# Step orders of their own for each layer and the first head pair, and earlier gate evictions, in a two-layer hybrid decoder trunk

## The chip, the cores and the metric

The kernel runs on one core of one Trainium2 chip. The metric is the device time of one execution in microseconds (us). A core has five engines that run side by side and wait for each other by semaphores: TensorE (PE, matmuls and transposes), VectorE (DVE), ScalarE (ACT), GpSimd (POOL) and SyncE (SP, which here issues the weight transfers).

## What is computed

The trunk has two layers over 528 tokens, 16 meta tokens ahead of 512, with 1024 channels.

```python
for l in range(DEPTH):
    u = rms_norm(h, norm_mix[l])
    glu_in, q, k, v, gates = jnp.split(u @ w_in[l], SPLITS, axis=-1)
    a = (glu_in + b_glu[l]); a = a[..., :C_CONV] * jax.nn.sigmoid(a[..., C_CONV:])
    a = causal_depthwise_conv(a, conv_w[l], conv_b[l])              # 31 taps
    y_conv = jax.nn.silu(layer_norm(a, ...)) @ w_pw[l] + b_pw[l]
    q, k = (apply_rope(rms_norm(x), cos, sin) for x in (q, k))      # 8 heads x 2 components x 64
    o = diff_attention(q, k, v, lam)          # softmax(q0 k0) - lam * softmax(q1 k1), causal, times v
    y_attn = rms_norm(o, subln[l], SUBLN_EPS) * (1.0 - lam_init)
    g_conv, g_attn = jnp.split(gates, 2, axis=-1)
    h = h + (jax.nn.sigmoid(g_conv) * y_conv + jax.nn.sigmoid(g_attn) * y_attn) @ w_o[l]
    u = rms_norm(h, norm_mlp[l])
    h = h + jnp.square(jax.nn.relu(u @ w_up[l])) @ w_down[l]
```

## The kernel before

For more precision than one matmul gives, weights and activations are split into a high and a low part, and each product is three matmuls (high x high, high x low, low x high). GpSimd makes the low parts of the weight slabs (`w_lo`), and in the attention stages ScalarE the high ones (`w_hi`).

A layer runs in this order: the GLU (`A_GLU`); then five **stages** of attention; then the gates and the layer norm of the convolution; then the pointwise product (`A_PW`), the output product (`A_O`) and the MLP. Stage 0 has only the projection tiles of v, q and k for head pair 0. Stages 1 to 4 do the attention of head pair 0 to 3; stages 1 to 3 also hold the projection tiles of the next pair, and stage 4 holds the first eight of the 16 gate tiles. Below, "first" is stage 1, "middle" are stages 2 and 3, "last" is stage 4. Layer 0 has 15 projection tiles a stage (five token tiles of v, q and k), layer 1 has 14, since the meta tokens' queries are not needed there.

The names of the steps, in which the change is written, with h0 and h1 the two heads of the stage's pair:

- `tile` (T): one projection tile; T< and T> are its first and second half, between which other steps may stand. ScalarE evicts it (`b_evict`) where its second half stands in the order: v to `v_sb`, q and k to `raw` with their squares. Behind the eviction of the last tile of v, of q and of k ScalarE casts the high part of the slab after the next (`w_high_part`, L871), GpSimd subtracts (`split_low`, L503).
- `gate` (G): a quarter of a gate tile. The first eight use one bank pair in turn; each must be evicted by VectorE (`gate`, `sg`, L1227) before the next starts. Gate tiles 8 to 15, in the normalisation, alternate between two bank pairs.
- `q`, `k` (k0, k1): transposes of the roped q and k, evicted by ScalarE (high part) and VectorE (low part, `qk_evict`). GpSimd makes the first product of the rope (`turn`, L548 and L549), VectorE the rest (`rope`; rq and rk in the new tables), behind the statistics (`rope_stats`).
- `s` (s00, s01, s02 for h0, s10 to s12 for h1): scores of a group of query tiles; `m` their maxima on VectorE (`maxima`), `e` the exponentials on ScalarE. The next scores wait for the exponentials of those before, since they use the same banks.
- `c` (`combine`, L1167): VectorE subtracts the second softmax from the first, in SBUF.
- `t` (t00, t01, t10, t11): transposes of the combined matrix, evicted to `a_t` by ScalarE (L906); the second half reuses the banks of the first.
- `pv`: its product with v. ScalarE sums its squares, VectorE scales it (`subln`), and `y` is its transpose. `pv-`, `y-` and `sub-` belong to the head before.

TensorE, ScalarE and VectorE each run their steps strictly in the order in which they are written. `schedule(layer, stage)` gives the order of TensorE and ScalarE, from a table of positions (`after`: an even key is the middle of a tile, an odd one its end) that serves stages 1 to 3 of both layers alike. VectorE's order is written out in its block. Between the steps it works off the taps of the convolution that the GLU has left (`some_taps(n)`, L441, 182 of them a layer), one multiply-and-add over 512 tokens each; `ln_sums` behind the last tap releases the layer norm's sums. In the normalisation VectorE multiplies each of eight channel tiles (L1405), ScalarE applies silu and VectorE subtracts its high part (`silu_lo`, L1135).

Of the kernel before, what the change touches and what calls it, by code (L numbers as in the profile page):

```python
# [40 lines left out]
T = META + SEQ  # L41
# [127 lines left out]

def schedule(layer, stage):  # L170

    h0, h1, pair = 2 * stage - 2, 2 * stage - 1, stage - 1
    pv = [("pv", h0 - 1)] if stage > 1 else []
    y = [("y", h0 - 1)] if stage > 1 else []
    s = lambda h, n: [("s", h, n)]
    e = lambda h, n: [("e", h, n)]
    if stage == 4:  # L180
# [47 lines left out]
def build(nc, x_t, w_slabs, pvecs, rows_in, ident_in, mask_in, identb_in, out, h_spill):  # L228
    ctx = ExitStack()
    with ctx:  # L230
# [834 lines left out]
        def _(dve):  # L1065
# [167 lines left out]
            for layer in range(LAYERS):  # L1233
# [89 lines left out]
                for stage in range(5):  # L1323
                    h0, h1 = 2 * stage - 2, 2 * stage - 1
                    last = stage == 4
                    if stage == 0:
                        some_taps(30)
                        rope(layer, 0, 0)
                        some_taps(8)
                        continue  # L1330
# [7 lines left out]
                    some_taps(1)  # L1338
                    qk_evict(layer, stage - 1, "q")
                    some_taps(1)  # L1340
                    qk_evict(layer, stage - 1, "k", 0)
                    maxima(layer, h0, 0)
                    if last:
                        gate(layer, 1)
                        some_taps(1)
                        maxima(layer, h0, 1)
                        qk_evict(layer, 3, "k", 1)
# [20 lines left out]
                        for _ in taps:  # L1368
                            pass
# [167 lines left out]
```

How the kernel before makes its waits and increments, by code:

```python
    def mark(self, ins):  # L104
        ins.then_inc(self.sem, 1)
        self.n += 1
# [1 line left out]
    def link(self, ins, back=0):  # L108
        self.mark(ins)
        if self.off is not None or self.n > back:
            self.eng.wait_ge(self.sem, self.value(back))
# [9 lines left out]
def announce(eng, ins, sem, value):  # L122
    ins.then_inc(sem, 1)
    eng.wait_ge(sem, value)
# [257 lines left out]
        def a_wait(eng, layer, slab, tile, k, col):  # L383
            if col == 0:
                eng.wait_ge(a_full, k + ((layer * A_TILES + tile) // 2 + 1))
            else:
                eng.wait_ge(w_used, k + (layer * SLABS + slab + 1))
# [5 lines left out]
        def b_read_wait(eng, n):  # L394
            for k in range(2):
                eng.wait_ge(b_free[k], (n + 1 - k) // 2)
# [1 line left out]
        def round_wait(eng, n):  # L399
            for m in (n - 1, n):
                eng.wait_ge(t_free[m % 2], m // 2 + 1)
# [1 line left out]
        def pv_read_wait(eng, layer, hh):  # L404
            n = ROUND["pv", layer, hh]
            eng.wait_ge(t_free[n % 2], n // 2 + 1)
# [35 lines left out]
        def late_taps(chain, layer):  # L443
            for ch, k in LATE:
                chain.link(conv_tap(layer, 0, ch, k, k == EARLY and ch < EARLY_TILES, k == TAPS - 1), back=1)
                if k == TAPS - 1 and ch % 2 and ch < NT - 1:
                    part = r_inv2[:, META:T]
                    chain.eng.wait_ge(chain.sem, chain.value())
                    if ch == 1:
                        chain.link(nc.vector.tensor_tensor(part, conv[:, 0, META:T], conv[:, 1, META:T], ALU.add))
                    else:
```

## Time and profile before

| | |
|---|---|
| median of 3 runs | 1986.39 us (1983.84 to 1986.53) |
| the profiled execution's own time | 1983.29 us |
| its span, first to last instruction | 1981.5 us |
| mean granted TensorE clock | 0.978 |
| DMA | 79 GB/s over the span |

The profile is of one execution. The span is the time from the first to the last instruction of the program; the execution's own time lies around it. Busy time of an engine leaves out the time in which it waits. The granted clock of TensorE has two levels in the trace, 2.4 GHz (1.00) and 1.2 GHz (0.50).

### The profile page before, as it was taken

The numbers are of one execution on the slowest core, as the hardware profiler recorded it, in microseconds if no ns is written. First come the engines' busy times: TensorE is split into PE (matmuls) and PEld (weight loads), VectorE is DVE, ScalarE is ACT, GpSimd is POOL, SyncE is SP. The second block draws the span as 40 slices with busy tenths as digits, with TensorE's granted clock in tenths as the row PEclk, the third lists the DMA queues.
The fourth block names the chain that finished last, engine by engine and source line by source line (L and its number), as shares of the span: only waits on it lengthen the run. The fifth ranks groups of instructions, "written<-read, shape, count | busy, mean of one in ns | idle before, by whom it ended". The sixth has DMA issues, their size and how long they took to land. (4 is left out here: it accounts for less than half of the span.)

```text
span 1981.5 us, 34343 instructions
## 1 busy us (share of the span) xinstructions
PE 1872.2 (94%) x12950; PEld 1693.5 (85%) x12950; DVE 1278.1 (65%) x1823; ACT 559.3 (28%) x1721; POOL 1126.7 (57%) x1124
## 2 busy tenths in 40 slices
PE   5999999899899999999999988898998999999999
PEld 5998788788899999999989987787766778888887
DVE  7997877978564433334569979779885654434443
ACT  3124665534312210111111344555334122110100
POOL 5667443423666676666656564334236677676764
PEclk9999999999999999999999998999999999999999
DMA  4221111011222222222332211110113222322222
GB/s 148 104 86 62 40 50 43 30 57 43 108 93 98 86 85 86 103 89 99 107 107 85 86 65 44 43 43 22 64 43 109 105 85 85 106 85 106 86 92 78
DMA packets 23870, 156.37 MB, mean 79 GB/s; under 512 B 2896, under 2 KB 3280, under 8 KB 6096
## 3 DMA queue, kind: packets, MB, share of 16 engines
q1 hardware_dynamic: 21744, 147.01, 20.9%
q10 hardware_dynamic: 2016, 7.86, 1.1%
q8 instruction: 74, 1.21, 0.2%
q14 instruction: 36, 0.29, 0.0%
HBM read 150.59 MB, written 4.26 MB: 78 GB/s over the span
## 5 line engine op out<-in xcount | busy, mean ns | idle before, releaser
L588 PE MATMUL psum<-u,w_hi 128*128 128x264 f32 (+1 forms) x4480 | 919.3, 317 | 51.8 <-DVE sg L1227 22.6
L588 PEld LDWEIGHTS psum<-u,w_hi 128*128 128x128 f32 x4480 | 682.3, 190 | 110.4 <-issue 24.5
L496 POOL TENSOR_TENSOR w_lo<-w_raw,w_hi 128x512 fp32r<-128x512 f32 x448 | 643.7, 1466 | 9.3
L588 PE MATMUL psum<-u,w_lo 128*128 128x264 f32 (+1 forms) x2240 | 568.9, 314 | 0.0
L588 PEld LDWEIGHTS psum<-u,w_lo 128*128 128x128 f32 x2240 | 370.8, 190 | 25.6
L648 PE MATMUL psum<-w_hi,u 128*128 128x256 f32 (+1 forms) x1856 | 348.5, 289 | 0.0
L493 POOL TENSOR_TENSOR tick<-ones 128x1 f32<-128x1 f32 x112 | 25.5, 228 | 538.6 <-PE psum L588 531.7
L441 DVE SCALAR_TENSOR_TENSOR psum<-xg,pvec,psum 128x512 f32<-128x512 f32 x440 | 299.5, 750 | 4.1 <-DVE xg L1271 2.2
L648 PEld LDWEIGHTS psum<-w_hi,u 128*128 128x128 f32 (+1 forms) x1856 | 272.2, 177 | 8.3 <-issue 0.4
L648 PE MATMUL psum<-w_lo,u 128*128 128x256 f32 (+1 forms) x928 | 264.3, 285 | 0.0
L503 POOL TENSOR_TENSOR w_lo<-w_raw,w_hi 128x128 fp32r<-128x128 f32 x384 | 180.5, 510 | 92.0 <-ACT w_hi L871 92.0
L494 POOL TENSOR_SCALAR w_hi<-w_raw 128x2048 fp32r<-128x2048 f32 x112 | 214.8, 1917 | 0.0
L1447 DVE TENSOR_TENSOR relu<-relu 128x528 f32<-128x528 f32 (+1 forms) x64 | 80.7, 1261 | 199.8 <-ACT u L1045 102.2
L1043 ACT ACTIVATE relu<-psum 128x528 f32<-128x528 f32 (+1 forms) x64 | 38.7, 604 | 461.8 <-PE psum L588 461.8
L648 PEld LDWEIGHTS psum<-w_lo,u 128*128 128x128 f32 (+1 forms) x928 | 163.8, 176 | 4.1
L588 PE MATMUL psum<-hid_b,w_hi 128*128 128x264 f32 (+1 forms) x768 | 163.8, 322 | 0.0
L1466 DVE TENSOR_TENSOR down_tmp<-psum,r_inv 128x528 f32<-128x528 f32 (+1 forms) x64 | 44.8, 700 | 174.5 <-PE psum L588 172.9
L548 POOL TENSOR_TENSOR rtmp<-raw,tabs 128x640 f32<-128x640 f32 x16 | 26.0, 1622 | 190.5 <-ACT squares L862 188.5
L588 PEld LDWEIGHTS psum<-hid_b,w_hi 128*128 128x128 f32 x768 | 118.9, 188 | 11.6
L1467 DVE TENSOR_TENSOR h<-h,down_tmp 128x528 f32 (+1 forms) x64 | 97.1, 1517 | 10.3 <-DVE down_tmp L1466 10.3
L588 PE MATMUL psum<-hid_b,w_lo 128*128 128x264 f32 (+1 forms) x384 | 102.4, 321 | 0.0
L889 ACT ACTIVATE e<-psum,nb,q_scale 128x272 f32<-128x272 f32 (+4 forms) x144 | 83.9, 587 | 44.8 <-DVE nb L1152 44.8
(169 smaller groups left out, 2083.5 us busy)
## 6 DMA issues: line engine op xcount, KB each, us to landing
w_raw<-w_slabs SPq DMA_DIRECT2D x136, 1024.0 KB, 4.8
h<-x_t SPq DMA_DIRECT2D x4, 528.0 KB, 7.3
h<-x_t ACTq DMA_DIRECT2D x1, 2112.0 KB, 8.3
h_spill<-h ACTq DMA_DIRECT2D x8, 264.0 KB, 2.4
h<-h_spill ACTq DMA_DIRECT2D x1, 2112.0 KB, 8.5
out<-h SPq DMA_DIRECT2D x8, 256.0 KB, 2.0
rows<-rows ACTq DMA_DIRECT2D x2, 512.0 KB, 4.6
pvec<-pvecs ACTq DMA_DIRECT2D x2, 156.5 KB, 2.9
```

Source lines behind the costliest of these rows:

```text
L441: return nc.vector.scalar_tensor_tensor(out=done if ends else acc, in0=x, scalar=w, in1=done if begins else acc, op0=ALU.mult, op1=ALU.add)
L494: chain.link(nc.gpsimd.tensor_scalar(w_hi[:, b, :], w_raw[:, b, :], 1.0, 1.0, ALU.mult, ALU.mult))
L496: last = nc.gpsimd.tensor_tensor(w_lo[:, b, c:c + SLAB // 4], w_raw[:, b, c:c + SLAB // 4], w_hi[:, b, c:c + SLAB // 4], ALU.subtract)
L503: last = nc.gpsimd.tensor_tensor(w_lo[:, b, c:c + P], w_raw[:, b, c:c + P], w_hi[:, b, c:c + P], ALU.subtract)
L548: nc.gpsimd.tensor_tensor(t4[:, :, :, 0:H2], x4[:, :, :, H2:HD], mid4(tabs[:, x, 1, :, 0:H2], 4), ALU.mult)
L588: last = nc.tensor.matmul(psum[:, 2 * slot + j, 0:n], w[:, b, cut], src[:, part, kc, at0:at0 + n], start=(kc == 0 and m == 0), stop=(kc == ...
L648: last = nc.tensor.matmul(psum[0:tn, n % 2, 0:2 * P], u[:, part, kc, t0:t0 + tn], w[:, b, kc * 2 * P:(kc + 1) * 2 * P], start=(kc == 0 and ...
L889: ins = nc.scalar.activation(e[0:tn, c, E_OFF[i]:E_OFF[i] + w], psum[0:tn, banks[c], S_AT[i]:S_AT[i] + w], ACT.Exp, bias=nb[0:tn, c, i:i + ...
L1043: nc.scalar.activation(row(relu[:, j, :], layer), a_ps(layer, j), ACT.Relu).then_inc(a_free[j], 1)
L1447: link(V.tensor_tensor(relu2[:, lo:lo + n], relu[:, j, lo:lo + n], relu[:, j, lo:lo + n], ALU.mult))
L1466: announce(dve, V.tensor_tensor(row(down_tmp[:], layer), a_ps(layer, j), row(r_inv2[:], layer), ALU.mult), a_free[j], a_read(layer, A_MLP ...
L1467: ins = V.tensor_tensor(rown(h, ch, layer), rown(h, ch, layer), row(down_tmp[:], layer), ALU.add)
```

## The change

`schedule` reads the order of TensorE and ScalarE from a table of strings, `MATRIX_ORDER`, with an entry for each layer and for the first, the middle and the last stages; VectorE reads its order from `VECTOR_ORDER` (a number is that many taps, g a gate eviction), with an entry for stage 0 too. Stage 0 has 31 taps in layer 0 and 23 in layer 1 (38 before in both), the first stage 32 and 30, a middle stage 35 and 41 (33 before), the last one the rest. In the normalisation the evictions of gates 10 to 15 are spread differently. No instruction is added or removed.

```diff
+MATRIX_ORDER = [{"first": "T T T< q T> T k0 T s00 e00 T T s01 T< e01 T> T< s02 k1 e02 T> T< s10 t00 t01 e10 T> T< s11 e11 T> pv0 T< s12 T> T< e12 T> T< y0 T> T< t10 T> t11",
+     "mid": "T pv- T T T< q T> T< k0 T> s00 y- T< k1 e00 T> T s01 T< e01 T> T s02 T< e02 T> T s10 t00 T< t01 e10 T> pv0 s11 T< e11 T> s12 T< e12 y0 T> T t10 t11",
...
+    {"first": "q T T T T k0 T< s00 e00 k1 T> T< s01 e01 T> T s02 T< e02 T> T< s10 t00 t01 e10 T> T< s11 e11 pv0 T> s12 e12 T T T T< t10 t11 T> y0",
+     "mid": "pv- T T T< y- T> T< q T> T< k0 T> s00 k1 T< e00 T> s01 e01 T T s02 T< e02 T> T< s10 t00 t01 e10 T> T< s11 e11 pv0 T> s12 e12 T T< y0 T> T< t10 t11 T>",
...
+VECTOR_ORDER = [{"zero": "26 rq 5",
+     "first": "4 stats 1 rk q 1 k0 3 m00 5 m01 5 m02 k1 c0 m10 7 m11 2 rq m12 sub0 c1 4",
+     "mid": "stats 5 rk sub- 3 q 1 k0 m00 3 m01 6 m02 k1 3 c0 1 m10 10 m11 sub0 m12 1 rq c1 2",
...
+    {"zero": "17 rq 6",
+     "first": "3 stats 1 q rk 1 k0 m00 4 m01 1 k1 4 m02 3 c0 m10 m11 3 m12 4 sub0 c1 6 rq",
+     "mid": "stats sub- 1 rk q 3 k0 2 m00 4 m01 5 k1 1 m02 3 c0 1 m10 6 m11 6 m12 sub0 c1 4 rq 5",
+     "last": "stats 4 g 2 sub- rk q 2 k0 2 m00 g 4 m01 3 k1 g m02 2 c0 2 g 4 m10 3 g 3 m11 5 m12 sub0 g 3 c1 1 g 7 ln g"}]
...
 def schedule(layer, stage):
...
-        after = {-1: pv, 3: y, 4: [("q", pair)], 7: [("k", pair, 0)], 9: s(h0, 0), 10: e(h0, 0), 13: s(h0, 1), 14: e(h0, 1),
-                 16: s(h0, 2) + [("k", pair, 1)] + e(h0, 2), 19: s(h1, 0) + [("t", h0, 0)], 20: [("t", h0, 1)] + e(h1, 0), 21: [("pv", h0)] + s(h1, 1) + e(h1, 1),
-                 24: s(h1, 2) + e(h1, 2), 25: [("y", h0)], 27: [("t", h1, 0)], 28: [("t", h1, 1)]}
...
+    for name in MATRIX_ORDER[layer]["first" if stage == 1 else "last" if stage == 4 else "mid"].split():
...
                 for stage in range(5):
...
-                    some_taps(3 if last else 4)
-                    rope_stats(layer, stage - 1)
-                    if stage > 1:
-                        subln(layer, h0 - 1)
-                    if last:
-                        gate(layer, 0)
-                    rope(layer, stage - 1, 1)
...
+                    for name in VECTOR_ORDER[layer]["zero" if stage == 0 else "first" if stage == 1 else "last" if stage == 4 else "mid"].split():
...
                     if i:
                         silu_lo(layer, i - 1)
-                    if i in (2, 6):
-                        gate(layer, EARLY_GATES + 2 + i // 4)
+                    if i in (2, 3, 5):
+                        gate(layer, EARLY_GATES + (0, 0, 2, 3, 0, 4)[i])
                 silu_lo(layer, NT - 1)
-                for k in range(4, 8):
+                for k in range(5, 8):
                     gate(layer, EARLY_GATES + k)
```

Lines behind the tables have other numbers after the change: 14 more up to VectorE's order, fewer behind it. Three places as the built program has them.

VectorE in layer 0's normalisation, before, from the eviction of gate 10 (`sg`) to that of gate 11:

```order
L1227 TENSOR_TENSOR sg<-psum,r_inv 128x528
L1405 TENSOR_TENSOR conv<-conv,ln_rs 128x528
L1135 TENSOR_TENSOR cact<-conv,cact 128x528
L1405 TENSOR_TENSOR conv<-conv,ln_rs 128x528
L1135 TENSOR_TENSOR cact<-conv,cact 128x528
L1405 TENSOR_TENSOR conv<-conv,ln_rs 128x528
L1135 TENSOR_TENSOR cact<-conv,cact 128x528
L1405 TENSOR_TENSOR conv<-conv,ln_rs 128x528
L1135 TENSOR_TENSOR cact<-conv,cact 128x528
L1227 TENSOR_TENSOR sg<-psum,r_inv 128x528
```

and after, from the eviction of gate 10 to that of gate 12:

```order
L1241 TENSOR_TENSOR sg<-psum,r_inv 128x528
L1380 TENSOR_TENSOR conv<-conv,ln_rs 128x528
L1149 TENSOR_TENSOR cact<-conv,cact 128x528
L1241 TENSOR_TENSOR sg<-psum,r_inv 128x528
L1380 TENSOR_TENSOR conv<-conv,ln_rs 128x528
L1149 TENSOR_TENSOR cact<-conv,cact 128x528
L1380 TENSOR_TENSOR conv<-conv,ln_rs 128x528
L1149 TENSOR_TENSOR cact<-conv,cact 128x528
L1241 TENSOR_TENSOR sg<-psum,r_inv 128x528
```

The eviction of gate 11 stands one pair behind that of gate 10, where four stood between.

ScalarE at the end of layer 0's second stage, before: the last two k tiles (`raw` and its squares), with the copies of head 1's transposes (`a_t`) between them.

```order
L858 COPY raw<-psum 128x256
L862 ACTIVATE squares,ssq<-psum 128x64 x4
L906 COPY a_t<-psum 128x512 x2
L906 COPY a_t<-psum 128x256
L908 COPY a_t<-psum 16x16
L906 COPY a_t<-psum 16x512
L858 COPY raw<-psum 128x256
L862 ACTIVATE squares,ssq<-psum 128x64 x4
L871 CAST w_hi<-w_raw 128x2048
L924 ACTIVATE y,osq<-psum 16x128
```

and after:

```order
L872 COPY raw<-psum 128x256
L876 ACTIVATE squares,ssq<-psum 128x64 x4
L872 COPY raw<-psum 128x256
L876 ACTIVATE squares,ssq<-psum 128x64 x4
L885 CAST w_hi<-w_raw 128x2048
L920 COPY a_t<-psum 128x512 x2
L920 COPY a_t<-psum 128x256
L922 COPY a_t<-psum 16x16
L920 COPY a_t<-psum 16x512
```

All copies to `a_t` now stand behind the last tile's eviction and the cast of `w_hi`.

VectorE in layer 1's second stage around head 0's combination (`es`, `es_eps`, `er`, then `e`), before:

```order
L1146 TENSOR_REDUCE mx<-psum 128x2
L1152 SCALAR_TENSOR_TENSOR nb<-mx,q_scale 128x2
L1221 TENSOR_TENSOR qk<-psum,qk 128x512
L1160 TENSOR_TENSOR es<-es 128x2
L1161 SCALAR_TENSOR_TENSOR es_eps<-es 128x5
L1162 RECIPROCAL er<-es 128x5
```

and after:

```order
L1235 TENSOR_TENSOR qk<-psum,qk 128x512
L455 SCALAR_TENSOR_TENSOR psum<-xg,pvec,psum 128x512
L1160 TENSOR_REDUCE mx<-psum 128x2
L1166 SCALAR_TENSOR_TENSOR nb<-mx,q_scale 128x2
L455 SCALAR_TENSOR_TENSOR psum<-xg,pvec,psum 128x512 x3
L1174 TENSOR_TENSOR es<-es 128x2
```

Three taps (L455) stand between the maxima and the combination, and the eviction of k has moved ahead of the maxima.

## Rows read from the trace of the kernel before

**Rows 1.** The page: busy us, share of the span and instructions of each engine.

```profile
PE 1872.2 (94%) x12950; PEld 1693.5 (85%) x12950; DVE 1278.1 (65%) x1823; ACT 559.3 (28%) x1721; POOL 1126.7 (57%) x1124
```

**Rows 2.** TensorE's waits: what waited for what, us in total, times, longest.

```profile
PE psum L588 <- DVE sg L1227: 22.6, 11, 5.8
PE psum L695 <- DVE e L1167: 18.9, 9, 3.7
...
PE psum L719 <- DVE y L1196: 11.3, 4, 3.1
...
PE psum L733 <- DVE qk L1221: 9.4, 3, 4.9
```

**Rows 3.** Stretches by stage: length; busy PE, PEld, DVE, ACT, POOL; clock; DMA.

```profile
121.00:237.95 116.95, 111.22 (x932) 101.75 (x930) 99.78 (x173) 60.38 (x272) 72.12 (x120) 0.99 0.16 56
237.95:311.15 73.20, 68.53 (x578) 60.37 (x578) 60.80 (x127) 43.39 (x187) 31.43 (x61) 1.00 0.13 44
311.15:387.50 76.35, 71.38 (x577) 63.24 (x576) 60.22 (x125) 43.31 (x187) 26.96 (x53) 0.96 0.12 43
387.50:471.70 84.20, 75.78 (x602) 67.92 (x601) 68.34 (x138) 26.92 (x101) 29.88 (x35) 0.98 0.14 51
471.70:534.00 62.30, 57.13 (x411) 55.42 (x412) 43.35 (x51) 32.45 (x47) 32.90 (x23) 0.95 0.16 55
1108.50:1225.75 117.25, 106.54 (x860) 98.77 (x859) 100.42 (x166) 56.17 (x240) 62.01 (x95) 0.94 0.16 56
1225.75:1302.20 76.45, 66.58 (x529) 59.94 (x526) 62.77 (x119) 39.83 (x160) 28.48 (x53) 0.93 0.12 42
1302.20:1379.50 77.30, 67.41 (x529) 61.09 (x528) 61.83 (x119) 39.63 (x160) 28.11 (x53) 0.93 0.12 42
1379.50:1464.90 85.40, 74.86 (x385) 57.19 (x383) 70.57 (x131) 24.08 (x80) 28.78 (x36) 0.92 0.14 50
1464.90:1527.00 62.10, 55.87 (x217) 41.41 (x218) 42.99 (x50) 31.53 (x46) 32.90 (x23) 0.95 0.19 66
```

**Rows 4.** Timeline, layer 1: two combinations on VectorE, GpSimd's rope product. Start, us.

```profile
1188.53 4.56 DVE L1167 SCALAR_TENSOR_TENSOR e<-e,er 128x144 f32<-128x144 f32 x4
...
1214.56 2.01 DVE L1167 SCALAR_TENSOR_TENSOR e<-e,er 128x144 f32<-128x144 f32 x4
...
1188.91 1.80 POOL L548 TENSOR_TENSOR rtmp<-raw,tabs 128x640 f32<-128x640 f32 x1 [8.54 <-ACT squares L862]
```

**Rows 5.** TensorE: timeline around waits; three gate tiles as in rows 3.

```profile
516.00 1.25 PE L588 MATMUL psum<-u,w_hi 128*128 128x264 f32 x4 [5.17 <-DVE sg L1227]
...
1193.15 1.97 PE L695 MATMUL psum<-ident,e 128*128 128x128 f32 x8 [3.68 <-DVE e L1167]
...
1216.62 1.09 PE L695 MATMUL psum<-ident,e 128*128 128x128 f32 x8 [0.94 <-DVE e L1167]
...
493.04:510.83 17.79, 17.78 (x145) 17.57 (x144) 16.42 (x15) 12.33 (x17) 14.10 (x9) 1.00 0.16 60
```

**Rows 6.** VectorE's timeline in layer 0's normalisation.

```profile
503.53 0.70 DVE L1227 TENSOR_TENSOR sg<-psum,r_inv 128x528 f32<-128x528 f32 x1
...
515.25 0.69 DVE L1227 TENSOR_TENSOR sg<-psum,r_inv 128x528 f32<-128x528 f32 x1
...
518.11 0.71 DVE L1135 TENSOR_TENSOR cact<-conv,cact 128x528 fp32r<-128x528 f32 x1 [0.81 <-ACT cact L1016]
```

**Rows 7.** Groups of layer 0's second stage: count, busy us, mean ns, idle before.

```profile
L648 PE MATMUL psum<-w_hi,u 128*128 128x256 f32 (+1 forms) x240 | 44.1, 285 | 0.0
...
L441 DVE SCALAR_TENSOR_TENSOR psum<-xg,pvec,psum 128x512 f32<-128x512 f32 x29 | 19.9, 752 | 0.2
L889 ACT ACTIVATE e<-psum,nb,q_scale 128x272 f32<-128x272 f32 (+4 forms) x20 | 11.2, 561 | 4.2 <-DVE nb L1152 4.2
...
L1146 DVE TENSOR_REDUCE mx<-psum 128x2 f32<-128x544 f32 (+4 forms) x10 | 6.8, 712 | 6.8 <-PE psum L683 6.8
```

**Rows 8.** ScalarE's timeline at the end of layer 0's first stage.

```profile
234.12 1.92 ACT L871 CAST w_hi<-w_raw 128x2048 fp32r<-128x2048 f32 x1
```

More of the change, by code:

```diff
@@ new lines @@
+MATRIX_ORDER = [{"first": "T T T< q T> T k0 T s00 e00 T T s01 T< e01 T> T< s02 k1 e02 T> T< s10 t00 t01 e10 T> T< s11 e11 T> pv0 T< s12 T> T< e12 T> T< y0 T> T< t10 T> t11",
[5 rows of a table added]
+VECTOR_ORDER = [{"zero": "26 rq 5",
[7 rows of a table added]
+def schedule(layer, stage):
+    h0, pair = 2 * stage - 2, stage - 1
+    if stage == 0:
+        return [("tile", j, None) for j in range(len(b_tiles(layer)))]
+    steps, tiles = [], iter(range(len(b_tiles(layer))))
+    gates = iter([(k, part) for k in range(EARLY_GATES) for part in range(4)])
+    for name in MATRIX_ORDER[layer]["first" if stage == 1 else "last" if stage == 4 else "mid"].split():
+        what, arg = name.rstrip("012-<>"), name.lstrip("GTpvqksety")
+        hh = h0 - 1 if arg == "-" else h0 + int(arg[0]) if arg and arg not in "<>" else h0
+        if what == "T":
+            if arg != ">":
+                j = next(tiles)
+            steps.append(("tile", j, {"<": 0, ">": 1, "": None}[arg]))
+        elif what == "G":
+            steps.append(("gate", *next(gates)))
+        elif what == "q":
+            steps.append(("q", pair))
+        elif what == "k":
+            steps.append(("k", pair, int(arg)))
+        elif what in ("pv", "y"):
+            steps.append((what, hh))
+        else:
+            steps.append((what, hh, int(arg[1])))
+    if stage == 4:
+        steps.append(("last y", HEADS - 1))
@@ new lines, in _ @@
+                    h0, gates = 2 * stage - 2, iter(range(EARLY_GATES))
+                    for name in VECTOR_ORDER[layer]["zero" if stage == 0 else "first" if stage == 1 else "last" if stage == 4 else "mid"].split():
+                        what, arg = name.rstrip("012-"), name.lstrip("kmcsub")
+                        if name.isdigit():
+                            some_taps(int(name))
+                        elif name == "stats":
+                            rope_stats(layer, stage - 1)
+                        elif name == "rk":
+                            rope(layer, stage - 1, 1)
+                        elif name == "rq":
+                            rope(layer, stage, 0)
+                        elif name == "q":
+                            qk_evict(layer, stage - 1, "q")
+                        elif what == "k":
+                            qk_evict(layer, stage - 1, "k", int(arg))
+                        elif what == "m":
+                            maxima(layer, h0 + int(arg[0]), int(arg[1]))
+                        elif what == "c":
+                            combine(layer, h0 + int(arg))
+                        elif what == "sub":
+                            subln(layer, h0 - 1 if arg == "-" else h0 + int(arg))
+                        elif name == "g":
+                            gate(layer, next(gates))
+                        elif name == "ln":
+                            for _ in taps:
+                                pass
+                            ln_sums()
```

80 lines of the change are left out of this document (removed), and 3 rows, old and new, of tables (MATRIX_ORDER, VECTOR_ORDER).

## The prediction, made before the change was run

> **What bounds the kernel now.** I read the page's busy times first. TensorE is busy 94% of the span, VectorE 65%, GpSimd 57%, ScalarE 28% [rows 1]. So only TensorE's idle time can be won, plus what its clock gives away. The list of who waited for whom then says on what it waits [rows 2]: VectorE's gate evictions (22.6 us), the combined exponentials of a head (18.9), the scaled head output y (11.3) and VectorE's eviction of q (9.4, of which one wait of 4.9). None of these is a DMA. The third view, busy time by stretch [rows 3], puts these in places. Each row is one stage: the first has the initial tiles and head pair 0, the next two the middle pairs, the fourth the last pair with its gate tiles, the fifth the normalisation; then the same five for layer 1. Window less busy time is idle: 5.7, 4.7, 5.0, 8.4 and 5.2 us in layer 0; 10.7, 9.9, 9.9, 10.5 and 6.2 in layer 1. Together 76.2 us. The rest of the kernel is untouched.
>
> The granted clock adds to this. The two middle stages of layer 0 hold the same matmuls, yet the second is busy 2.85 us longer, at a clock of 0.96 against 1.00 [rows 3]. After a wait of 3.68 us eight transposes take 1.97 us, after one of 0.94 us they take 1.09 [rows 5]: the lower level, 1.2 GHz, follows the longer waits. I charge 1.7, 0, 2.85, 1.7 and 2.4 us to the five stages of layer 0, and 4.4, 4, 4, 5.6 and 1.4 to layer 1's, from the mean clock of each row (0.93 of 76.45 us is 5.4 us of clock, of which part falls on idle time). So 76.2 + 28.1 = 104 us is the ceiling.
>
> **The gate evictions, part one of the change.** After the last matmul before it at 510.8, TensorE stood 5.17 us before 516.00, waiting for a gate eviction [rows 5]. Gate tiles alternate between two bank pairs, so tile 13 needs tile 11 evicted. VectorE did that at 515.25, behind four multiply-and-subtract pairs, while an eviction takes 0.70 us [rows 6]. The new order puts it one pair behind the eviction at 503.53, thus at about 505.6, just after tile 11 is complete (504.9: a gate tile takes 5.9 us, three of them 17.8 [rows 5]), and tile 12's two pairs later, at about 512.4. Tile 13 then starts at once, and tile 14, 5.9 us later, finds 12 evicted. The same evictions are done in all, and what they delay is the chain of silu products, which ends at 518.8 now [rows 6] and near 520 then; its first reader, the pointwise product behind gate tiles 13 to 15, cannot start before 510.8 + 3 x 5.9 = 528.5. The cover is 8 us; if it were gone, the 5.2 us would come back there. Gain in layer 0: 5.17 + 2.4 = 7.6. Layer 1 has 6.2 idle, of which a wait of 0.4 for tile 10 stays, and 1.4 of clock: 7.2.
>
> **The orders, part two.** No instruction is added or removed, so I lay each stage out by the durations of the rows: a tile 2.9 us (44.1 for 15), a tap 0.67 to 0.75, and from scores to the next scores two to three maxima of 0.71 and exponentials of 0.56, about 4.1 to 4.7 us in a row [rows 7]. A wait is what such a chain exceeds the tiles put beside it.
>
> *Layer 0, first stage.* The eviction of q now stands ahead of fewer taps (stage zero has 31, not 38), so the 4.2 us before the first k transposes fall to about 1. Smaller waits at the first transposes (0.5 + 0.4), a score (0.6) and the values (0.4) remain: 7.4 becomes 3.0, gain 4.4.
>
> *Layer 0, middle stages.* y of the previous head has now four tiles instead of two behind its values: its waits (11.3 us in four, two of them here) go. Three things return. (1) Three taps stand ahead of head 0's combination, so it runs when GpSimd starts its rope product. The same four instructions took 4.56 us beside GpSimd and 2.01 alone [rows 4]; I take 1.7 us of wait. (2) Head 1's second and third scores have one tile between them, 2.9 us for a chain of 4.1: 1.1. (3) The transposes of head 1 are now both behind the last tile, and ScalarE's copies of them behind that tile's eviction (1.2) and the cast of the next weights, 1.92 us [rows 8]. The second transposes need the banks of the first: 1.2 + 1.9 + 1.1 of copies against 1.6 of work is 2.9 with what follows. Each stage 5.7; two are 11.4 against 12.5 before, gain 1.1.
>
> Here a page speaks against the change. The Trainium skill, "SBUF — State Buffer", in its table of ports and their consequences, says that a VectorE instruction with two SBUF inputs contends with a GpSimd one that reads SBUF. The trace agrees [rows 4]; by the rule in full, without the part that I let run before GpSimd starts, each combination would cost the whole 2.55 us, and the sum would lose some 3 us.
>
> *Layer 0, last stage.* 10.1 before; after it the first gate still waits for the chain of statistics, rope and y (2.65), then 0.85, 0.7, 0.5 and 0.7 at values, a gate and the final transposes: 5.4, gain 4.7.
>
> *Layer 1, first stage.* q's transposes come four tiles ahead of k's. Statistics, q eviction and rope of k end at about 1160.8 where TensorE arrives at 1160.1. The 4.9 becomes 0.7; the 3.7 at the combination, which no longer meets GpSimd, becomes about 1.9; 1.9 more for scores and transposes. 15.1 becomes 4.5, gain 10.6.
>
> *Layer 1, middle stages.* Before: 9.9 + 4 each. Now subln stands directly behind the statistics and y behind 2.5 tiles, no wait in the first and 1.6 in the second stage. The combination still meets GpSimd: 2.2 for 3.7. Scores, transposes 0.5 each, four times. But taps rise from 33 to 41, 5.4 us more VectorE work on 62.8 busy [rows 3], so VectorE is full; I add 1.0 for a sum of conv channels that falls badly and 1.7 of clock. 27.8 becomes 13.2 for the two, gain 14.6.
>
> *Layer 1, last stage.* The nine taps and the rope that end the middle order now delay statistics, gate 0 and k: 1.2, 1.0, 2.8, 1.8 and 2.0, 0.8 for the rest and 1.7 of clock, 11.4 for 16.1: gain 4.7.
>
> **The sum.** 4.4 + 1.1 + 4.7 + 7.6 + 10.6 + 14.6 + 4.7 + 7.2 = 54.9 us. The profiled execution took 1983.3 us around its 1981.5 us span: 1928.4 by the profile. The median of three runs is 1986.4, 3.1 us above that execution; taken from it, 1931.5, I say 1932. A change within 0.2% (4 us) could not be told from none.
>
> Bounds of what the trace doesn't show: the collisions and the VectorE load. Below: half of the waits that I let stand in the middle and last stages (11.4 + 5.4 + 13.2 + 11.4) go too, 20.7 us more gain, 1911. Above: all of the second part but the two first stages is lost: 7.6 + 7.2 + 4.4 + 10.6 = 29.8 of gain, 1956.
>
> **The rivals.**
> - *VectorE becomes the bound* (0.17): more taps per middle stage, and every combination beside GpSimd. For it: 62.8 busy plus 5.4 is already the 67 us that a stage of layer 1 would take. Against: the last stages give taps back. Then only the first stages and the gates gain, 1956.
> - *The waits nearly vanish* (0.20): the collisions are missed by a microsecond, since all producers shift with the consumers. About 1911 to 1921.
> - *The change does nothing in the end* (0.03): it needs every order to be as good as the old, and the gate chain to stall at the silu products instead. 1983 to 1990.
> - *Slower: the clock* (0.03). The new order has many waits of 1 to 3 us, two of them close together at the end of each middle stage of layer 0. If each such pair brings the lower level, it costs about 1.4 us (2.85 for the two pauses of that stage [rows 3]). It decides from 39 such drops (54.9 / 1.4), in a program that has under half as many. With 45 of them: 1995.
> - My forecast, 1922 to 1944: 0.57.
>
> From these the range 1913 to 1953 leaves out 2 in 10. Faster 0.94, same 0.03, slower 0.03.
>
> **What the profile after would show.** Right: no TensorE wait over 1 us in either normalisation, TensorE's busy time lower by 15 to 25 us at an unchanged number of matmuls, VectorE idle under 5 us in layer 1's middle stages; a wait of 1.5 to 3 us ahead of the last transposes in layer 0's middle stages, released by ScalarE; combinations of 4 to 5 us there. Wrong: a wait of over 3 us for y or for the q eviction, a gap ahead of the pointwise product's first tile, or a mean clock as low as before in layer 1.

## The result and the profile after

The changed kernel takes 1966.43 us (median of 4 runs, 1966.08 to 1971.02), the kernel before 1986.1 us beside it: a ratio of 0.9909, 95% interval 0.9895 to 0.9924. It is faster, by some 20 us (18 by the ratio), where I had forecast 55. One execution of the later variant `all_three` (2051.33 us) and one of the kernel before beside `values_later` (4017.2 us) were far slower than their neighbours, and the times and ratios below leave them out. The profiled execution has a span of 1965.0 us against 1981.5, at a mean granted clock of 0.979 against 0.978.

The page's busy times, to be held against [rows 1]:

```profile
PE 1876.9 (96%) x12950; PEld 1691.1 (86%) x12950; DVE 1277.4 (65%) x1823; ACT 557.7 (28%) x1721; POOL 1129.3 (57%) x1124
```

TensorE's busy time has risen by 4.7 us over the same 12950 matmuls; I had named 15 to 25 us less as a sign that the forecast was right. TensorE's waits, as in [rows 2]:

```profile
PE psum L709 <- DVE e L1181: 19.5, 10, 3.6
...
PE psum L689 <- ACT e L903: 5.6, 7, 1.4
PE psum L709 <- ACT a_t L920: 4.7, 9, 1.1
PE psum L733 <- DVE y L1210: 4.4, 4, 2.0
PE psum L753 <- DVE y L1210: 4.1, 2, 3.4
PE psum L602 <- DVE sg L1241: 4.0, 7, 1.5
```

The gate evictions fell from 22.6 to 4.0 us, y from 11.3 to 4.4. The combined exponentials did not fall at all (18.9 to 19.5). One row is new: the transposes of q (L753), which read `raw`, wait for VectorE's scaled output y, 3.4 us at worst. The stages, cut as in [rows 3] (the normalisation now up to the first matmul of the pointwise product):

```profile
122.90:242.20 119.30, 114.55 (x956) 104.03 (x953) 101.20 (x173) 60.25 (x272) 78.42 (x129) 0.99 0.16 55
242.20:326.85 84.65, 74.61 (x578) 65.07 (x577) 68.36 (x132) 43.22 (x187) 37.07 (x66) 0.92 0.13 44
326.85:403.85 77.00, 70.58 (x554) 61.21 (x553) 63.79 (x129) 43.30 (x187) 30.06 (x52) 0.92 0.12 41
403.85:485.60 81.75, 78.20 (x601) 70.21 (x601) 63.16 (x129) 24.48 (x89) 28.49 (x24) 0.94 0.15 51
485.60:543.10 57.50, 57.50 (x431) 55.72 (x431) 41.15 (x51) 34.34 (x58) 25.73 (x18) 0.98 0.18 65
1115.30:1227.00 111.70, 105.91 (x861) 97.31 (x860) 86.79 (x147) 55.71 (x240) 57.97 (x94) 0.97 0.17 59
1227.00:1299.30 72.30, 65.13 (x529) 57.59 (x527) 67.65 (x124) 39.73 (x160) 28.53 (x54) 0.98 0.13 45
1299.30:1377.75 78.45, 71.01 (x551) 61.98 (x548) 73.42 (x143) 40.02 (x160) 33.73 (x68) 0.98 0.12 41
1377.75:1455.65 77.90, 68.66 (x359) 52.13 (x360) 64.04 (x122) 21.82 (x71) 26.32 (x22) 0.91 0.16 55
1455.65:1509.70 54.05, 54.05 (x219) 40.16 (x218) 41.91 (x50) 33.21 (x54) 29.13 (x21) 1.00 0.20 66
```

Three cuts don't hold quite the same work. A tile (2.9 us) has moved from layer 0's third stage to its first, and a gate tile (5.8 us) from layer 1's last stage to its third. With that set right, layer 0's first stage changed by -0.5 us, its middle ones by +11.5 and +3.5, its last by -2.4; layer 1's by -5.6, -4.2, -4.7 and -1.7. The normalisations gained 7.0 and 7.9 us (from the channel sums to the pointwise product), and are free of idle time. What got longer is layer 0's middle stages, the first of them above all: 10.0 us idle where there were 4.7, and a clock of 0.92 where there was 1.00. That is not the whole miss: every attention stage also gained less than forecast (below).

TensorE's timeline there, and at the end of the next stage:

```profile
252.94 1.94 PE L753 MATMUL psum<-ident,raw 128*128 128x128 f32 x8 [3.44 <-DVE y L1210]
...
390.32 1.09 PE L709 MATMUL psum<-ident,e 128*128 128x128 f32 x8 [1.50 <-DVE e L1181]
392.48 1.73 PE L709 MATMUL psum<-ident,e 128*128 128x128 f32 x7 [1.06 <-ACT a_t L920]
394.92 8.39 PE L721 MATMUL psum<-v_sb,a_t 16*128 16x128 f32 x28 [0.71 <-ACT a_t L920]
```

And VectorE's timeline ahead of the first of these waits:

```profile
234.97 1.44 DVE L1103 TENSOR_SCALAR nw_y<-nw_v 128x40 int32<-128x40 int32 x1
236.45 1.48 DVE L1104 SCALAR_TENSOR_TENSOR nw_a<-nw_y 128x40 f32<-128x40 f32 x1
237.96 0.38 DVE L1105 TENSOR_TENSOR nw_a<-nw_a,nw_v 128x40 f32<-128x40 f32 x1
...
240.71 3.38 DVE L455 SCALAR_TENSOR_TENSOR psum<-xg,pvec,psum 128x512 f32<-128x512 f32 x5
244.00 2.22 DVE L1130 TENSOR_TENSOR raw<-raw,tabs 128x1280 f32<-128x1280 f32 x1
...
251.69 1.11 DVE L1210 TENSOR_SCALAR y<-psum,nw_y 128x128 f32<-128x128 f32 x4
```

The bank into which q is transposed is the one that held the previous head's values. It is free when `sub-` (`subln`, L1210) has read it. In the old order `sub-` stood right behind the statistics; in the new one five taps (3.4 us) and k's rope (5.5 us) stand ahead of it, behind statistics that take 6.1 us. `sub-` ends at 252.80, and TensorE starts at 252.94. I had followed y to its own reader, the transpose of y, and not the bank to its next writer.

### The profile page after: what moved, and what is told of

It is laid out like the page before. It is cut to its first block and busy times, and to the rows that moved or that the text cites. A ratio compares the mean times of both kernels' runs of the same rounds, so it can differ in the third digit from the quotient of the medians.

```text
span 1965.0 us, 34360 instructions
## 1 busy us (share of the span) xinstructions
PE 1876.9 (96%) x12950; PEld 1691.1 (86%) x12950; DVE 1277.4 (65%) x1823; ACT 557.7 (28%) x1721; POOL 1129.3 (57%) x1124
## 5 line engine op out<-in xcount | busy, mean ns | idle before, releaser
L455 DVE SCALAR_TENSOR_TENSOR psum<-xg,pvec,psum 128x512 f32<-128x512 f32 x440 | 300.9, 750 | 4.1 <-DVE xg L1285 2.2
```

The costliest lines, as they stand in the source:

```text
L455: return nc.vector.scalar_tensor_tensor(out=done if ends else acc, in0=x, scalar=w, in1=done if begins else acc, op0=ALU.mult, op1=ALU.add)
```

## The experiments

All times are compared with the kernel before, run on the same chip; "ratio" is to it, with the 95% interval.

**The parts apart.** First the two parts of the change, each alone, then the new orders for one layer at a time (both with the new gate evictions). The edit of `gates_only` is the third hunk of the diff alone, that of `orders_only` all but it; the other two put the old order, written as a table, in one entry:

```diff
 (new_layer1)
-MATRIX_ORDER = [new layer 0, new layer 1]; VECTOR_ORDER = [new layer 0, new layer 1]
+MATRIX_ORDER = [old order, new layer 1]; VECTOR_ORDER = [old order, new layer 1]
 (new_layer0)
+MATRIX_ORDER = [new layer 0, old order]; VECTOR_ORDER = [new layer 0, old order]
```

> The orders of attention as before in both layers, with only the gate evictions of the normalisation moved. Main theory (the parts add up; the new orders lose in layer 0 and win in layer 1): the 7.0 and 7.9 us that the two normalisations got shorter between the traces belong to this part alone, so about 1971 us, 15 below before. Rival (the evictions gain only because the new orders bring another clock and another phase into the normalisation): under 5 us gain, 1982 or more.

Measured 1970.86 us, ratio 0.993 (0.9911 to 0.995).

> Both new tables of orders, with the gate evictions where they were. Main theory: layer 0's attention is 12 us longer and layer 1's 16 us shorter, so about 4 us below before, 1982; TensorE waits over 5 us in both normalisations again. Rival (the parts do not add up): 1975 or less.

Measured 1981.24 us, ratio 0.9983 (0.9974 to 0.9993).

> The changed kernel, but with layer 0 in the orders of before. Main theory: it lacks the 12 us that layer 0's new orders cost and keeps all gains, so about 1954 us, 12 below the changed kernel. Rival (the loss in layer 0 is a matter of where the clock's lower level happened to fall in the one profiled execution): within 4 us of the changed kernel, 1962 to 1970.

Measured 1957.32 us, ratio 0.9869 (0.9848 to 0.9891): 9 us faster than the changed kernel.

> The changed kernel, but with layer 1 in the orders of before. Main theory: before less 15 for the gates plus 12 for layer 0, 1983 us. Rival (the loss of layer 0 is chance in one execution): 1971 to 1975.

Measured 1980.33 us, ratio 0.9974 (0.9962 to 0.9987).

The evictions alone give 14 us (0.7%), some three quarters of the 18 us that the change brings by its ratio, and the orders 3.4 us (0.17%). The orders split into two of opposite sign: against the evictions alone, layer 1's gain 12 us (0.993 to 0.9869) and layer 0's cost 9 us (0.993 to 0.9974).

**Repairs of layer 0's middle stages.** One for each wait: `sub-` ahead of rope; the head-1 transposes moved apart; the combination ahead of the taps, this one in both layers. `all_three` has the three edits together, and `all_four` to `all_six` further down each build on the one before.

```diff
 (sub_first)      VECTOR_ORDER[0]["mid"]
-stats 5 rk sub- 3 q 1 k0
+stats 5 sub- rk q 4 k0
 (tail)           MATRIX_ORDER[0]["mid"]; VECTOR_ORDER[0]["mid"]
-T t10 t11        m12 1 rq c1 2
+T< t10 T> t11    m12 1 c1 rq 2
 (combine_first)  VECTOR_ORDER[0]["mid"]; VECTOR_ORDER[1]["mid"]
-k1 3 c0 1        m02 3 c0 1
+k1 c0 4          m02 c0 4
```

> The changed kernel; in layer 0's middle stages VectorE scales the previous head (sub-) ahead of k's rope and evicts q right behind that rope: 'stats 5 sub- rk q 4 k0' for 'stats 5 rk sub- 3 q 1 k0'. Main theory: the first middle stage's wait of 3.44 us ahead of q's transposes is for the bank that sub- frees, so it goes, with some 2.9 us of lower clock behind it; the second middle stage had no such wait. About 1960 us, 6 below the changed kernel (ratio to before 0.988). Rival (VectorE has too much work there, and what is taken from one wait goes to the next): a wait of over 2 us ahead of k's transposes or of the first scores, 1964 or more.

Measured 1968.08 us, ratio 0.9907 (0.9892 to 0.9922). The 3.44 us wait is gone, and two others stand in its place, for k's transposes and for the first scores:

```profile
253.60 0.39 PE L745 MATMUL psum<-ident,raw 16*128 16x16 f32 x4 [0.48 <-DVE qk L1233]
...
257.58 1.43 PE L687 MATMUL psum<-qk 64*128 64x272 f32 x24 [1.40 <-DVE qk L1227]
```

By the time the rival held (1964 or more), though the waits that came are under its 2 us: with k's rope moved behind `sub-`, k and the scores wait. This speaks for VectorE being late in this place as a whole, and not in one step.

> The changed kernel; in layer 0's middle stages head 1's first transposes stand in the middle of the last tile instead of behind it, and the second ones behind it, and VectorE combines ahead of the rope of the next q: 'T< t10 T> t11' and 'm12 1 c1 rq 2'. Main theory: the waits of 1.50 and 1.06 us (and 0.71 at the values ahead of the last stage) come from the rope ahead of the combination and from ScalarE's cast ahead of its copies. Both middle stages lose them, some 5 us with the lower clock behind them up to 8 more: about 1957 us (0.985). Rival (the combination can't be ready half a tile sooner): 2 us or more of wait at the first transposes remain, 1964 or more.

Measured 1972.76 us, ratio 0.9932 (0.9919 to 0.9946): a miss, and by 0.0023 of ratio slower than the changed kernel. The transposes' first wait fell to 0.73 us, but ScalarE's cast of the next weights now stands ahead of the second copies to `a_t`, and the values waited 3.03 us for them; the second middle stage got its own wait for q's bank (2.98 us).

> The changed kernel; in the middle stages of both layers VectorE combines head 0 right behind its maxima, and the three taps that stood ahead of it follow: 'c0 4' for '3 c0 1'. Main theory: the combination then ends before, or soon after, GpSimd starts its rope product, so its long instructions take 2 to 3 us in place of 4.6 to 4.9, and the waits at the next transposes (2.62, 1.74 in layer 0, 3.57, 3.10 in layer 1) fall below 1 each: 8 us less, with the lower clock that follows three of them 12 less, about 1955 us (0.984). Rival (the combination is slow for another reason than GpSimd's work, or the taps then hold back the maxima of head 1 by as much): 1962 or more.

Measured 1960.93 us, ratio 0.9874 (0.9857 to 0.9891): 5.5 us better (7 by the ratios), half of the 11 expected, and 1 us short of the rival's band. In layer 0 the waits of 2.62 and 1.74 us ahead of head 0's transposes are gone; in layer 1 the combination met GpSimd's turning in its new place too, and 3.08 and 2.48 us of wait stayed.

> The three edits together, each as in its own kernel. Main theory: they remove different waits and add up, 6 + 8 + 11: about 1941 us (0.977). Rival (VectorE full: the waits move from one step to the next): the sum is under 15 us, 1952 or more.

Measured 1958.8 us, ratio 0.9853 (0.9833 to 0.9874), a miss: 1941 was expected, and the rival's band (1952 or more) held. Layer 0's first middle stage is repaired: 72.9 us long, 4.4 idle, none of it at the lower clock. The next one lost it again, at the values, which ran from end to end at 1.2 GHz:

```profile
382.44 8.39 PE L719 MATMUL psum<-v_sb,a_t 16*128 16x128 f32 x28 [3.03 <-ACT a_t L918]
```

**The clock at the end of a stage.** In the changed kernel the trace grants 1.2 GHz from 391.96 us for 13.65 us, from within the second of the waits of 1.50, 1.06 and 0.71 us shown above. Does moving the values behind two gate quarters save it?

```diff
 (values_later)  MATRIX_ORDER[0]["last"]
-pv- G G G G q G k0
+G G pv- G G q G k0
```

> The changed kernel, with two gate quarters ahead of the first layer's last values instead of behind them (G G pv- G G q in place of pv- G G G G q). Theory, that TensorE's lower clock after the third head pair is set off by the cluster of waits of 1.50, 1.06 and 0.71 us at 390 to 395 us: the 0.71 us wait ahead of the values goes, the stretch at the lower clock (13.65 us from 391.96) is cut to 3 to 7 us, the values take about 5.1 us instead of 8.92, and the kernel takes 1961 to 1963 us against 1966.4. Rival, that the lower clock follows from something else in that stretch (the transposes' two waits alone): the low stretch stays near 13 us, only moved onto gate quarters, and the time stays at 1965 to 1967.

Measured 1968.27 us, ratio 0.9914 (0.99 to 0.9928). The low stretch fell to 3.41 us and the values to 4.74 us; so far the theory held:

```profile
397.61 4.74 PE L719 MATMUL psum<-v_sb,a_t 16*128 16x128 f32 x28
...
407.81 1.06 PE L751 MATMUL psum<-ident,raw 128*128 128x128 f32 x8 [2.03 <-DVE y L1208]
```

But the values' bank is again the one that q needs next, and later values mean a later `sub-`: 2.03 us of new wait, and 1.2 GHz comes back at 409.19 (3.41 us) and for 10.24 instead of 6.83 us from 477. The time did not move.

> The three repairs of the middle stages together, with the values two gate quarters later as well. Theory, that the three of them gave 6 us and that the 13.65 us at the lower clock on the last values are the largest thing left in the first layer: the wait of 3.03 us ahead of these values falls to under 1.2, the values take about 5.1 us instead of 8.39, and the time is 1951 to 1955 us against 1960.3 with three. Rival, that the next step pays instead (q for the last pair stands two quarters closer to its channel sums and bank): 1958 to 1962.

Measured 1956.07 us, ratio 0.9856 (0.984 to 0.9872). By ratio it is no better than `all_three`: on the same work (two gate quarters, 2.9 us, have moved) the third stage is 6.2 us shorter and the last one 6.5 us longer, 5.90 us of it a wait for that same bank.

```diff
 (all_five)  VECTOR_ORDER[0]["last"]
-2 stats 3 rk sub- 1 g
+2 stats 3 sub- rk 1 g
 (all_six)   as all_five, and MATRIX_ORDER[1]["mid"]
-T> T< s10 t00 t01 e10 T> T< s11
+T> T< s10 T> t00 t01 e10 T< s11
```

> The kernel with the three repairs and the later values (1956.1 us), and in the first layer's last stage VectorE's normalisation of the values ahead of k's part of RoPE (sub- rk in place of rk sub-). Theory, that the 5.90 us wait of q's transposes at 395.6 us is the bank that this normalisation frees, 3.2 us late behind RoPE: the wait falls to 2 to 3 us, and the time to 1951 to 1953 us. Rival, that k's scores then wait for RoPE by as much: 1955 to 1957.

Measured 1957.95 us, ratio 0.9868 (0.9853 to 0.9883). The wait fell to 2.02 us, and the first gate quarter behind it waited 4.82 us for its eviction.

> The same again, and in the second layer's two middle stages half an input tile moved from behind the e transposes to ahead of them (T< s10 T> t00 t01 e10 T< s11 in place of T< s10 t00 t01 e10 T> T< s11). Theory, that the transposes' waits of 2.47 and 3.12 us there are for VectorE's combination beside GpSimd's turning and can be covered by work: each falls by about 1.4 us, and the time by 2 to 3 us against all_five, 1948 to 1950 us. Rival, that the second head's scores or their exponentials wait in their place: no difference to all_five within 1 us.

Measured 1963.9 us, ratio 0.9903 (0.9885 to 0.992): 7 us slower than `all_five` by the ratios. The waits for the combination fell by 2.0 and 1.4 us, and the next scores waited 2.84 us each time for ScalarE's exponentials, which are due later by as much.

> The first layer's orders as before the change, the second's new with its combination taken right behind the last maxima, the gates' evictions as changed. Theory, that the new orders pay in the second layer and cost in the first, and that the combination is worth a little in the second: 1953 to 1957 us (the same without the earlier combination took 1957.3). Rival, that the second layer's earlier combination does nothing, since it ran 4.85 us beside GpSimd wherever it stood: 1957 to 1959.

Measured 1957.7 us, ratio 0.986 (0.9844 to 0.9876), not to be told from `new_layer1` (0.9869), as the rival had it.

Seven further orders for layer 0, and the best of them (0.9853 and 0.9856) only draw level with the old order there (0.986). What moved was always the place of the wait. That left the question why VectorE was late at all.

**GpSimd beside VectorE.** First its many short subtractions are cut down, then the turning for rope, then both.

```diff
 (no_low_parts)  split_low
-for c in range(0, SLAB, P):
+for c in range(SLAB - P, SLAB, P):
 (small_turn)    turn
-nc.gpsimd.tensor_tensor(t4[:, :, :, 0:H2], x4[:, :, :, H2:HD], ...)      # and its second half
+few = NTOK if (pair, x) == (0, 0) else 1
+nc.gpsimd.tensor_tensor(t4[:, 0:few, :, 0:H2], x4[:, 0:few, :, H2:HD], ...)
 (small_both)    both edits
 (old_small_turn) the edit of small_turn on the kernel before
```

> The changed kernel, of whose subtractions for the weights' low parts GpSimd runs only the last of every 16 in the attention stages (the output is then not the reference's). Theory, that VectorE's small and three-operand instructions are slowed by GpSimd's beside them and so end late: the combination takes 2.0 us instead of 2.1 to 4.9 for its long instructions, the statistics under 4.5 us instead of 6.1 to 6.9, TensorE's waits of 3.44, 2.62 and 1.74 us in the first layer and of 2.90, 3.57 and 3.10 us in the second fall to under 1 us each, and the kernel takes 1935 to 1950 us. Rival, that VectorE is late by the number of its instructions and not by GpSimd's: those waits keep over half their length, and the time stays above 1955.

Measured 1953.11 us, ratio 0.9832 (0.9816 to 0.9848). The gain of 13 us is real, but of the six waits named the four for the combination stayed: 2.62 and 1.73 us in layer 0, 3.11 twice in layer 1 (3.57 and 3.10 were expected to go). The 3.44 became 2.26, and layer 1's 2.90 became 0.98. The subtractions are not what holds the combination up.

> The changed kernel, in which GpSimd turns only the first of the five token tiles for RoPE (all five for each layer's very first q, so that the rest of the tile holds numbers; the output is then not the reference's). Theory, that the combination's small instructions (up to 1.58 us each for 5 elements) are held up by GpSimd's two long instructions of the turning: the combination takes 2.0 to 2.5 us from its first three-operand instruction, TensorE's waits of 2.62 and 1.74 us in the first layer and 3.57 and 3.10 us in the second fall under 1 us each, the wait of 3.44 us stays over 2, and the kernel takes 1952 to 1958 us against 1966.4. Rival, that the combination comes late by its place in VectorE's queue: the waits stay over half their length and the time above 1961.

Measured 1936.29 us, ratio 0.9751 (0.9726 to 0.9776): 30 us under the changed kernel, well past what I expected. Head 0's waits for the combination are gone in layer 0's middle stages and 1.05 us each in layer 1's, and the 3.44 us for q's bank, expected to stay over 2, fell to 1.06.

> The changed kernel with both of GpSimd's works cut: the last of every 16 subtractions for the low parts, and one of five token tiles turned (the output is not the reference's). Theory, that the two prices add (13 us and about 11 us), and that the rest above the forecast of 1932 us is the order's own (q's bank, waits of 1.4 us, the clock behind them): 1938 to 1946 us. Rival, that nearly all of the miss is GpSimd's: 1930 to 1936. Second rival, that the two overlap and the second gives little on top of the first: 1947 to 1953.

Measured 1932.62 us, ratio 0.9741 (0.9726 to 0.9756). The prices don't add; the second gives 2 to 4 us on top of the first. That this is my forecast's number is chance, as the next run shows.

> The kernel before the change, in which GpSimd turns only the first of five token tiles for RoPE (all five for each layer's very first q; the output is then not the reference's). Theory, that the new orders put VectorE's short instructions beside the turning where the old ones did less: before falls by less than 15 us, from 1984 to 1969 to 1980, and the changed orders then gain 33 to 44 us without the turning, near the forecast of 55. Rival, that the kernel before pays as much for it: it falls by 25 to 30 us, to 1954 to 1959, the changed orders gain some 20 us either way, and the miss is not the turning's.

Measured 1962.55 us, ratio 0.989 (0.9873 to 0.9906): the kernel before gains 22 us by the same cut. So the changed orders and evictions are worth 0.9751/0.989 = 0.986, 28 us, without the turning and 18 us by the ratio with it. Neither of my two bands held; it lies nearer to the rival. The turning explains about 10 us of the miss of 35, an estimate from three ratios that is good to some 7 us either way. It lies in layer 0's middle stages. First those of `old_small_turn`, then of `small_turn`:

```profile
236.65:310.50 73.85, 70.08 (x577) 61.97 (x578) 59.89 (x126) 43.49 (x187) 26.99 (x61) 0.98 0.12 44
310.50:384.80 74.30, 69.91 (x578) 61.84 (x577) 59.54 (x129) 43.23 (x187) 22.80 (x53) 0.98 0.12 44
```

```profile
238.10:313.85 75.75, 70.42 (x577) 61.06 (x577) 63.50 (x130) 43.20 (x187) 31.30 (x63) 0.98 0.17 56
313.85:386.20 72.35, 67.66 (x554) 59.39 (x553) 57.27 (x127) 43.32 (x187) 23.64 (x52) 0.97 0.11 35
```

With the turning the two stages take 149.6 us before [rows 3] and 161.7 after; without it 148.2 and 148.1 (the moved tile's 2.9 us come on top of both figures of after). The old order loses 1.4 us to the turning there, the new one 13.6.

**The same turning in short instructions.** Why the turning hurts can be seen at head 0's combination in the changed kernel, VectorE's timeline and GpSimd's:

```profile
283.18 1.58 DVE L1175 SCALAR_TENSOR_TENSOR es_eps<-es 128x5 f32<-128x5 f32 x1
...
284.90 1.35 DVE L1177 SCALAR_TENSOR_TENSOR er<-er,lam,es 128x5 f32<-128x5 f32 x1
...
283.17 1.57 POOL L562 TENSOR_TENSOR rtmp<-raw,tabs 128x640 f32<-128x640 f32 x1 [10.16 <-ACT squares L876]
284.70 1.52 POOL L563 TENSOR_TENSOR rtmp<-raw,tabs 128x640 f32<-128x640 f32 x1
```

An instruction over five elements takes 1.58 us: it starts with one GpSimd instruction and ends with it, and the next one ends with the other. So I cut the turning by token tiles:

```diff
 (turn_in_tiles)  turn
-nc.gpsimd.tensor_tensor(t4[:, :, :, 0:H2], ...)
-nc.gpsimd.tensor_tensor(t4[:, :, :, H2:HD], ...).then_inc(turned, 1)
+for j in range(NTOK):
+    nc.gpsimd.tensor_tensor(t4[:, j:j + 1, :, 0:H2], ...)
+    last = nc.gpsimd.tensor_tensor(t4[:, j:j + 1, :, H2:HD], ...)
+last.then_inc(turned, 1)
```

> The changed kernel, its turning cut into five pairs of 128x128 instructions in place of one pair of 128x640 (same work, same output). Theory, that VectorE's instructions with two operands in on-chip memory wait for the GpSimd instruction that runs (1.58 us for 5 elements from 283.18, while the 1.57 us of turning ran from 283.17): each such wait falls to 0.3 to 0.4 us, the combination beside the turning from 5.6 us to some 3.5, and the kernel takes 1952 to 1960 us against 1966.4. Rival, that VectorE is slowed in proportion to GpSimd's work beside it: the turning takes as long, and the time stays within 3 us of 1966.4 or rises by GpSimd's 8 further instructions.

Measured 1951.75 us, ratio 0.9826 (0.9813 to 0.9839): 14.7 us faster than the changed kernel with the same work, and the fastest kernel of this study with the reference's output. The theory's range (1952 to 1960) held to within 0.3 us, and the rival's (within 3 us of 1966.4) did not. The same combination, VectorE and GpSimd:

```profile
280.49 0.17 DVE L1177 SCALAR_TENSOR_TENSOR es_eps<-es 128x5 f32<-128x5 f32 x1
...
280.79 0.22 DVE L1179 SCALAR_TENSOR_TENSOR er<-er,lam,es 128x5 f32<-128x5 f32 x1
281.05 2.30 DVE L1183 SCALAR_TENSOR_TENSOR e<-e,er 16x16 f32<-16x16 f32 x5
...
280.49 0.50 POOL L563 TENSOR_TENSOR rtmp<-raw,tabs 128x128 f32<-128x128 f32 x1 [10.11 <-ACT squares L878]
...
281.36 2.31 POOL L563 TENSOR_TENSOR rtmp<-raw,tabs 128x128 f32<-128x128 f32 x1
```

The short ones take 0.17 and 0.22 us. Now GpSimd waits in turn: one of its instructions, 0.46 us elsewhere, takes 2.31 us across VectorE's five subtractions. TensorE's waits for the combination fell from 19.5 to 11.2 us. The wait for q's bank did not fall: it is 4.60 us here, and ahead of it the first long instruction of k's rope takes 5.55 us where it took 2.22:

```profile
239.09 5.55 DVE L1132 TENSOR_TENSOR raw<-raw,tabs 128x1280 f32<-128x1280 f32 x1
...
236.22 6.69 POOL L517 TENSOR_TENSOR w_lo<-w_raw,w_hi 128x128 fp32r<-128x128 f32 x16
```

## Why the forecast was wrong in size

By its own steps, from the trace:

- **The gate evictions** were right: 7.6 and 7.2 us forecast, 7.0 and 7.9 measured, both long waits gone, and 14 us when changed alone.
- **By stage** the forecast missed 3.9 us in layer 0's first stage, 16.1 in its two middle ones and 2.3 in its last, and 5.0, 5.8 and 3.0 in layer 1's. Less than half of the miss is in layer 0's middle stages.
- **The idle time** came out 8.4 us short: of 76.2 us I let some 46 stand, that is 30.2 of gain, and 54.4 stand (the windows less their busy time), 21.8 of gain. In layer 1 the combination waited 3.57 and 3.10 us where 2.2 each was in the sum, and k's first transposes 2.90 us where 0.7 was. The waits that I foresaw in layer 0's middle stages came: 1.7 at the combination was 2.62 and 1.74, 1.1 at the scores was 1.39, and 2.9 at the tail was 1.50 + 1.06 + 0.71.
- **The step that failed first** is "its waits go. Three things return" in layer 0's middle stages. A fourth returned, the wait of 3.44 us for the bank that `sub-` frees. The forecast took rope and statistics at the durations of the old order, and counted each moved step for its reader alone. A wait of over 3 us for y was on my list of signs that the forecast is wrong; it came, at another reader than I meant.
- **The term that was mis-sized most** is the clock. 28.1 us were charged to it before, and the sum left 3.4, so 24.7 of the 54.9 us were to come from it. Busy time rose by 4.7 us instead. In the first 600 us the trace has 47.8 us at 1.2 GHz where there were 27.3, and around layer 1's attention (1000 to 1540 us) 34.1 where there were 61.4; but what was saved there had lain in good part on idle time. In layer 0's middle stages alone busy time rose by 8.2 us (6.1 and 2.1, the moved tile counted) where a gain of 2.85 was in the sum: 11 of the miss. The last and first stages of both layers gave back 0.6 us or less, or lost up to 2.4, where 11.7 were counted. I had treated the lower clock as the tail of a long wait that goes with it. But the new orders left clusters of waits of 0.7 to 1.5 us. At one such cluster the values took 8.39 us, where the same 28 matmuls took 4.74 at the full clock.
- Together: 8.4 us of idle time, 24.7 of clock not gained and 4.7 lost are 37.8 of the 38.4 us between the profile's sum (1928.4) and its time with this change (1981.5 - 16.5 = 1965.0 of span, and 1.8 around it as before).
- **Behind a part of both** stands VectorE's lateness. Short instructions with all operands in SBUF ran beside the turning. I had priced this at the combination alone and by the long instructions, 4.56 against 2.01 us [rows 4]. It also struck the statistics: two took 1.44 and 1.48 us beside the turning of 234.76 to 237.86 us, and 0.33 and 0.41 in `small_turn`. In the old order eight taps lay there, one operand of each in PSUM, and took their usual 0.67 us apiece:

```profile
231.91 5.36 DVE L441 SCALAR_TENSOR_TENSOR psum<-xg,pvec,psum 128x512 f32<-128x512 f32 x8
...
234.49 1.54 POOL L548 TENSOR_TENSOR rtmp<-raw,tabs 128x640 f32<-128x640 f32 x1 [17.53 <-ACT squares L862]
236.00 1.54 POOL L549 TENSOR_TENSOR rtmp<-raw,tabs 128x640 f32<-128x640 f32 x1
```

- **The page** that I weighed (the Trainium skill, "SBUF — State Buffer", Who interferes with whom) says that a VectorE instruction with two SBUF inputs contends with a GpSimd instruction that reads SBUF. The trace agrees: 1.58 us against 0.17 for one over five elements. The price was above the some 3 us that I had weighed for it, since the cut of the turning gave 30 us on the changed kernel and 22 on the one before. The time at 1.2 GHz over the span fell with it, from 81.9 to 58.0 us and from 88.7 to 71.7.
- **The rivals.** "VectorE becomes the bound" named the right engine, but its condition was wrong: VectorE is busy 68 of 85 us in the worst stage, late and not full. "Slower: the clock" had the right mechanism at too small a price and chance: a cluster cost not 1.4 us but, at its worst, 3.7 us on the values alone (8.39 against 4.74).
- **The sum itself** has a slip: the terms written for layer 1's middle stages give 12.7 us at the nearest, or 13.4 if the last two are counted in each stage, not 13.2. It moves the sum by 0.5 us at most.

What stays open: some 25 us of the miss of 35 are still there with the turning cut. The larger part of them is lower clock that was not won back: between `old_small_turn` and `small_turn` TensorE's busy time falls by 3.2 us (1869.4 to 1866.2), where 24.7 were booked. Why it isn't won back was not tested. Also why the clock of layer 0's last stage fell to 0.94 with half the former idle time (3.55 against 8.4 us) was not tested; and the new order of layer 0 with the turning in short instructions and `sub-` early together, which the 4.60 us wait suggests, was not run.

## What to carry to other kernels

When a step is moved, follow three things: who reads its result, who writes next into the buffer that it frees, and what GpSimd runs in its new place. Put VectorE's PSUM work beside GpSimd's long instructions and its short SBUF work elsewhere, or cut the GpSimd instruction into short ones, which here cost GpSimd 23 us of busy time over the kernel (1129.3 to 1152.3), while the kernel got 14.7 us faster. Be wary of booking a gain of clock where waits are only shortened: here a cluster of waits of 0.7 to 1.5 us kept the lower level, and it fell on full matmuls.

## What the runs showed of the hardware that was not expected

A VectorE instruction over five elements took 1.58 us, as long as the GpSimd instruction that started 10 ns ahead of it, against 0.17 us in all 16 executions of the kernel before; a GpSimd instruction of 0.46 us took 2.31 us across five of VectorE's in a row. Each of the two seems to hold the other off for whole instructions, and not to halve its rate. The fences above show this at one place, and the 14.7 us that shorter instructions gave speak for it over the kernel. With them, one long VectorE instruction (128x1280) took 5.55 us beside GpSimd's row of subtractions where it had taken 2.22.

The lower level of the clock was granted for 13.65 us around waits of 1.50, 1.06 and 0.71 us, from within the second, while TensorE was busy but for these; with the last of them gone it was 3.41 us (`values_later`). The length isn't fixed by the waits: around the same three, within 0.06 us, it was 13.65 us in `sub_first` too, 10.24 in `combine_first` and `no_low_parts`, and 6.83 in `small_turn` and `turn_in_tiles`, where the same values took 6.27 and 6.54 us. What decides between these was not tested.
